# Rows for the PE inside and behind the expert mixing, early row fetches on POOL, and reordered evacuations and softmax products in a two-block transformer kernel

## What is computed

```python
q = (h @ wq).reshape(B, S, 8, 2, 128)
sub_scores = einsum('bshpk,hpnk->bshpn', q, subkeys)      # 2 x 128 scores for each head
top_v, top_i = top_k(sub_scores, 16)
cand = top_v[..., 0, :, None] + top_v[..., 1, None, :]    # 256 candidates
best_v, best_pos = top_k(cand, 16)                        # 16 of 16384 experts
gates = softmax(best_v)
hid = gelu(einsum('tkd,td->tk', u[expert], x)) * gates
out = einsum('tk,tkd->td', hid, v[expert])
```

## Time and profile before

| | |
|---|---|
| median of 3 runs | 3134.32 us (3134.2 to 3149.95) |
| the profiled execution, its own time | 3133.42 us |
| its span | 3131.7 us |
| PE busy | 2735.1 us, 87% |
| PE weight loads | 2092.0 us, 67% |
| DVE busy | 1690.6 us, 54% |
| ACT busy | 898.5 us, 29% |
| POOL busy | 1306.2 us, 42% |
| moved by DMA | 584.37 MB, mean 187 GB/s |
| mean granted clock of TensorE | 0.941 of full speed |

### The profile page before, as it was taken

One profiled execution on the slowest core, in us unless ns is written; L12 is line 12 of the kernel. 1 busy time (PEld: TensorE's weight loads), 2 busy tenths in 40 slices (PEclk: granted clock), 3 DMA queues, 4 the chain that ended last, 5 costly groups with the idle time before them and its releaser, 6 DMA issues.

```text
span 3131.7 us, 32456 instructions
## 1 busy us (share of the span) xinstructions
PE 2735.1 (87%) x12138; PEld 2092.0 (67%) x12138; DVE 1690.6 (54%) x3212; ACT 898.5 (29%) x1634; POOL 1306.2 (42%) x979
## 2 busy tenths in 40 slices
PE   7989997899997889999896789999999799999800
PEld 6856886678787668887775678888888644444300
DVE  1032044843225244340315646999966999666699
ACT  3264244423334232222325233111113920000000
POOL 3422434634445224434342132344444544444574
PEclk9999998999998999999998799999999999999955
DMA  4300332013233116563331032899999089999997
GB/s 152 100 7 21 95 93 69 1 41 94 81 114 122 54 47 208 175 194 115 88 96 47 1 108 98 311 388 391 383 366 399 1 300 380 403 409 410 409 408 285
DMA packets 216990, 584.37 MB, mean 187 GB/s; under 512 B 23921, under 2 KB 48642, under 8 KB 216322
## 3 DMA queue, kind: packets, MB, share of 16 engines
q1 hardware_dynamic: 137312, 301.22, 28.2%
q0 software_dynamic: 74688, 271.61, 22.2%
q10 hardware_dynamic: 4834, 9.46, 0.9%
HBM read 574.88 MB, written 7.35 MB: 186 GB/s over the span
## 4 chain that ended last, share of the span: by engine, by line
PE 63%; DVE 13%; DMA 11%; issue 5%; ACT 4%; POOL 4%; SPq 0%; DVEq 0%; ACTq 0%; POOLq 0%
PE ps L1152 13%; PE ps L1154 13%; PE ps L1153 13%; PE ps L1601 12%; DMA rows<-in_v,expert 5%; DMA rows<-in_u,expert 5%; POOL rows L1086 3%; DVE ps L2256 1%; PE ps L1118 1%; DVE hg L2285 1%; DVE hot L2274 1%; PE ps L1230 1%; DVE rows L2244 1%; PE ps L1170 1%; PE ps L1168 1%
## 5 line engine op out<-in xcount | busy, mean ns | idle before, releaser
L991 POOL TENSOR_TENSOR wlo<-wraw,whi 128x1024 fp32r<-128x1024 f32 x258 | 621.3, 2415 | 974.0 <-ACT whi L543 973.9
L543 ACT ACTIVATE whi<-wraw 128x1024 fp32r<-128x1024 f32 x258 | 271.1, 1058 | 852.3 <-PE ps L1154 747.8
L1626 PE MATMUL ps<-stream,hg 128*128 128x512 f32 x1024 | 441.8, 594 | 7.7 <-DMA stream<-in_v 6.9
L1152 PE MATMUL ps<-hhi,whi 128*128 128x512 f32 x1096 | 431.8, 394 | 18.9 <-DVE hlo L1735 6.7
L1601 PE MATMUL ps<-haff,stream 128*128 128x256 f32 x2048 | 444.1, 380 | 2.2 <-ACT stg L928 2.2
L1154 PE MATMUL ps<-hhi,wlo 128*128 128x512 f32 x1096 | 429.4, 392 | 0.0
L1153 PE MATMUL ps<-hlo,whi 128*128 128x512 f32 x1096 | 429.0, 391 | 0.0
L1601 PEld LDWEIGHTS ps<-haff,stream 128*128 128x128 f32 x2048 | 390.1, 191 | 55.7 <-ACT stg L928 2.4
L1626 PEld LDWEIGHTS ps<-stream,hg 128*128 128x128 f32 x1024 | 195.1, 191 | 253.8 <-issue 245.1
L2244 DVE CUSTOM_DVE_ANT_0 rows<-rows,h_s 128x1024 f32<-128x1024 f32 x256 | 313.5, 1225 | 83.6 <-DMA rows<-in_u,expert 78.1
L1086 POOL DMA_INDIRECT rows<-in_v,expert x256 | 244.8, 956 | 270.9 <-DVE ps L2256 119.1
(11 more groups left out here) (447 smaller groups left out, 4089.7 us busy)
## 6 DMA issues: line engine op xcount, KB each, us to landing
stream<-in_ut SPq DMA_DIRECT2D x128, 512.0 KB, 6.8
stream<-in_v SPq DMA_DIRECT2D x128, 512.0 KB, 6.8
wraw<-in_w_in SPq DMA_DIRECT2D x96, 512.0 KB, 3.6
wraw<-in_w_ada SPq DMA_DIRECT2D x48, 512.0 KB, 4.0
wraw<-in_w_gu SPq DMA_DIRECT2D x88, 256.0 KB, 3.8
wraw<-in_w_down SPq DMA_DIRECT2D x22, 512.0 KB, 3.5
wraw<-in_w_br_ssm SPq DMA_DIRECT2D x16, 512.0 KB, 3.5
wraw<-in_w_xkv SPq DMA_DIRECT2D x16, 512.0 KB, 4.2
```

The source lines that it names most:

```text
L543: act.activation(whi[:, n % WSLOTS, 0:kn, :], wraw[:, n % WSLOTS, 0:kn, :], ACT.Copy).then_inc(w_hi, 1)
L991: pool.tensor_tensor(wlo[:, n % WSLOTS, 0:kn, :], wraw[:, n % WSLOTS, 0:kn, :], whi[:, n % WSLOTS, 0:kn, :].bitcast(F32), ALU.subtract).th ...
L1152: pe.matmul(dst, lh, rh, start=k == 0, stop=False)
L1626: ins = pe.matmul(ps[:, 2 * i + half, :], hg[:, n, P * i:P * i + P], stream[j][:, 4 * half:4 * half + 4, :], start=n == 0, stop=n == NKEYS ...
```

## The change

The sixteen rows of block 12 (v of tile 0), of which the ring holds eight when the hole begins, are handled by the PE inside the hole: a diagonal matrix of the token weights times the row buffer, in two halves of 512 columns, every fourth batch a whole row. ACT makes the first four diagonals between the gelus of dense tiles 126 and 127, DVE the other twelve between batches, and POOL issues fetches between its one-hots, for which it has four buffers of its own. In blocks 28, 30 and 31 the odd ranks are handled by the PE in the same way, with diagonals by ACT, while DVE sums the even ones; tile 0 and the dense tiles are finished after block 28, their root and scaling stand between later rows, and tile 1 alone is behind the last row. Modulation vector 5 moves from behind `gu10` to behind `gu4`. The memory is transposed to the banks of `mix0`, and `xk0`, `xk1` are evacuated before parts of the normalization of x. The cross-attention issues scores three tiles ahead. In the sliding window ACT makes diagonals of the reciprocals, and a matmul with them takes the place of multiplication and transpose. On POOL, `after("pq0")`, the first eight fetches and `after("pq3")` replace `after("pq3")`; the loads of the dense tiles' scores follow.

```diff
-GELU_AT = {21: 0, 40: 1, 66: 2, 91: 3, 110: 4}
+GELU_AT = {21: 0, 40: 1, 66: 2, 91: 3, 107: 4, 118: 5}
+PE_HOLE = [(12, k) for k in range(TOPK)]
+PE_TAIL = [(b, k) for b in (28, 30, 31) for k in range(1, TOPK, 2)]
+DIAGS, POOL_HOTS = 4, 4
+ENDS = (0, 2, 3, 1)
+VECTORS = [(i,) for i in range(4)] + [(4, 5)] + [(i,) for i in range(6, 12)]
...
             for i in range(NT):
                 u_root_of(i)
+            group(G["xk0"], (0, 1), to_features(kx, 0, n=MEM))
             for i in range(NT):
                 x_square(1, i)
+            group(G["xk1"], (0, 1), to_features(kx, 4, n=MEM))
             for i in range(NT):
                 x_root_of(i)
-            for i in range(2):
-                group(G[f"xk{i}"], (0, 1), to_features(kx, 4 * i, n=MEM))
...
+            def sw_diagonals(b):
+                act.wait_ge(s("sw_rec"), b + 1)
+                if b:
+                    act.wait_ge(s("sw_tr"), 4 * b)
+                for h in range(SW_HEADS):
+                    act.activation(sw_dg[:, h, :], ident, ACT.Copy, scale=srec[:, h:h + 1]).then_inc(s("sw_p"), 1)
...
+            def row_diags(mine):
+                for b, k in mine:
+                    r = PE_ROWS.index((b, k))
+                    act.wait_ge(s("wrow_ready"), PE_BLOCKS.index(b) + 1)
+                    if r >= DIAGS:
+                        act.wait_ge(s("pe_row_used"), r - DIAGS + 1)
+                    n = TOPK * BLOCKS[b][2] + k
+                    act.activation(diag[:, r % DIAGS, :], ident, ACT.Copy, scale=wrow[:, n:n + 1]).then_inc(s("diag_ready"), 1)
...
+                if n == NKEYS - 2 and PE_HOLE:
+                    row_diags(PE_HOLE[:DIAGS])
...
+            if PE_TAIL:
+                row_diags(PE_TAIL[:8])
+                tile_squares((0, 1, 2))
+                row_diags(PE_TAIL[8:16])
+            row_gelu(1, PEER_HEADS - 1)
...
             after("out1")
-            after("pq3")
-
+            after("pq0")
...
+            for n in range(RING):
+                gather_next()
+            after("pq3")
             load_scores(0)
             load_scores(1)
-            for b, (kind, t, h) in enumerate(BLOCKS):
-                if kind == "u":
-                    pool.wait_ge(s("head_done"), top_done(t, h))
+            for b in range(len(BLOCKS)):
                 for k in range(TOPK):
                     if k == RING and b == MIX_AFTER + 1:
                         pool.wait_ge(s("slots_ready"), 1)
                         for m in range(ND // 4):
                             first_hot(m)
+                            if PE_HOLE and m % 4 == 0 and m > 4:
+                                gather_next()
...
-            xa_scores(0)
+            for i in range(3):
+                xa_scores(i)
...
+                    pe.wait_ge(s("sw_p"), SW_HEADS * b + 2 * n + 2)
                     for m in range(4):
...
-                        ins = transpose(ps[:, 4 + n, P * m:P * m + P], sw_ss[b % 2][:, q // 2, P * (q % 2):P * (q % 2) + P])
+                        ins = pe.matmul(ps[:, 4 + n, P * m:P * m + P], sw_ss[b % 2][:, q // 2, P * (q % 2):P * (q % 2) + P], sw_dg[:, q // 2, :], start=True, stop=True)
...
+            def row_half(r, half):
+                b, k = PE_ROWS[r]
+                mine = [n for n, (c, _) in enumerate(PE_ROWS) if BLOCKS[c][1] == BLOCKS[b][1]]
+                j, count = row_count(b, k)
+                if half == 0:
+                    pe.wait_ge(row_landed[j], 16 * count)
+                    pe.wait_ge(s("diag_ready"), r + 1)
+                return pe.matmul(ps[:, 6 + half, :], diag[:, r % DIAGS, :], rows[j][:, 512 * half:512 * half + 512], start=r == mine[0], stop=r == mine[-1])
...
+                if PE_HOLE and b % 4 == 1:
+                    row_half(b // 4, 0)
+                if PE_HOLE and b % 4 == 3:
+                    row_half(b // 4, 1).then_inc(s("pe_row_used"), 1)
...
+            def hole_diagonal(r):
+                b, k = PE_HOLE[r]
+                n = TOPK * BLOCKS[b][2] + k
+                v.wait_ge(s("pe_row_used"), r - DIAGS + 1)
+                v.tensor_scalar(diag[:, r % DIAGS, :], ident, wrow[:, n:n + 1], None, ALU.mult).then_inc(s("diag_ready"), 1)
...
+            between_rows = {(28, 14): lambda: later_weights(30), (30, 2): lambda: later_weights(31),
+                            (30, 8): lambda: root_begin((0, 1, 2)), (30, 14): lambda: root_end((0, 1, 2)),
+                            (31, 2): lambda: scaled_out((0,)), (31, 4): lambda: scaled_out((1,)), (31, 6): lambda: scaled_out((2,))}
...
                 if b == MIX_AFTER:
+                    if PE_HOLE:
+                        head_weights(*BLOCKS[PE_HOLE[0][0]][1:]).then_inc(s("wrow_ready"), 1)
...
+            if PE_TAIL:
+                link(add_tile(1, own_sums(1)))
+                v.wait_ge(s("pe_row_used"), len(PE_ROWS))
+                add_tile(1, row_sums(1)).then_inc(x_ready, 1)
```

More of the change, by code:

```diff
@@ L969, in scalar_program @@
                 row_gelu(0, h)
-            for h in range(PEER_HEADS):
+            for h in range(PEER_HEADS - 1):
                 row_gelu(1, h)
-            for i, t in enumerate((0, 2, 3, 1)):
-                act.wait_ge(x_ready, NT * 4 + i + 1)
-                act.activation(yout[:, t, :], xf[:, t, :], ACT.Square, accum_out=ssq[:, t:t + 1]).then_inc(usq_ready, 1)
-            act.wait_ge(usq_ready, part_count(4, 0, NT - 1))
-            root(meps)
+            if PE_TAIL:
[3 more added lines that the diff above has]
+            row_gelu(1, PEER_HEADS - 1)
+            if not PE_TAIL:
+                tile_squares((0, 1, 2, 3))
+            tile_root((0, 1, 2))
+            row_diags(PE_TAIL[16:])
+            if PE_TAIL:
+                tile_squares((3,))
+            tile_root((3,))
         def gpsimd_program(pool):
@@ L1366, in tensor_program @@
             pe.wait_ge(s("memn_ready"), 2)
-            evacuated("mix1")
+            evacuated("mix0")
             for k in range(KD):
                 for i in range(2):
-                    ins = transpose(ps[:, k, P * i:P * i + P], mem_n[:, i, P * k:P * k + P])
-                ins.then_inc(s("mtr_ready"), 1)
+                    ins = transpose(mem_t(k)[:, P * i:P * i + P], mem_n[:, i, P * k:P * k + P])
+                if k % 2:
+                    ins.then_inc(s("mtr_ready"), 1)
             pe.wait_ge(s("m_lo"), KD)
@@ L1628, in tensor_program @@
                 ins.then_inc(s("v_mm"), 1)
+            for r in range(len(PE_HOLE), len(PE_ROWS)):
+                row_half(r, 0)
+                row_half(r, 1).then_inc(s("pe_row_used"), 1)
         def vector_program(v):
```

243 lines of the change are left out of this document (155 added, 88 removed).

## The result

| | before | after |
|---|---|---|
| median of 20 runs | 3143.43 us (3133.87 to 3149.95) | 3125.78 us (3114.69 to 3134.67) |
| profiled execution, its span | 3131.7 us | 3118.6 us |

The ratio is 0.9948, with a 95% interval of 0.9934 to 0.9961: about 16 us faster, where 33 were forecast and the range ended at 3118. The direction was right, the size was not. Of the three runs that the prediction had of the kernel before, two (3134.2 and 3134.32 us) are among the fastest of its twenty and one (3149.95) is the slowest; the profiled execution, 3133.42 us, is faster than all twenty.

A forecast was written before the change was run, and what follows sets the result against it. It took PE to bound the kernel before about 1970 us and DMA to be full in the last 1150 us except the hole. Terms summed to -33.4 us, from 3133.42 to 3100.0 us, range 3080 to 3118.

The forecast's parts named there:

- memory and xk: Memory and cross-attention: earlier mem transposes, xk0 and xk1 evacuated first; -8 us (-2 to -10).
- the attention: Cross-attention: with three score tiles ahead, scores leave the turn for tiles 1 and 2; -3.3 us (-2 to -5).
- the stall at pq2: Start of pq2: PE idles 6.3 us for POOL's low part, then 1.9 more; +8.2 us (5 to 11).
- the hole's start: Start of the hole: ACT's four diagonals delay slot_t from 2415.37 to 2418.4; +3 us (0 to 5).
- length: Inside the hole: PE's row halves and DVE's twelve diagonals lengthen it; +5.5 us (2 to 15).
- the sliding window: Sliding window: DVE loses its multiplication, ACT gains diagonals, k_out's transposes start earlier; -12 us (-8 to -14).
- The hole's yield: After the hole: DVE stands 16 rows further on; -20.5 us (-18 if only the 14 fetches issued inside count).
- the tail: Last blocks: 14 us saved behind the last fetch, last landing slips 7 to 10; -6 us (-14 to +4).
- the early rows pay: Rival at pq and the DMA-bound stretches: eight early rows gain 10.3 us without PE stall; 3081.5 us, chance 0.06.
- the hole eats its yield: Rival in the hole: every half costs PE's whole 0.5 us, start and length +20.5; 3112 us, chance 0.14.
- TensorE's lower clock: Rival in the tail: TensorE at 1.2 GHz, a row 3.4 us on PE; 3117 us, chance 0.08.
- The slow hole: Rival: TensorE stays at 1.2 GHz through the hole, PE needs 170 us there; 3165 us, chance 0.03.

The follow-up runs named there:

- the first experiment: Changed kernel with the eight early fetches issued behind pq3's low parts; median 3123.97 us, span 9.6 us less once corrected for a differing start.
- the third experiment: Changed kernel with no rows for PE in the hole; median 3131.24 us, span 10.4 us more once corrected for a differing start.
- second experiment: Changed kernel with no rows for PE in blocks 28, 30, 31; median 3126.83 us, span 2.6 us less once corrected for a differing start.
- The seventh experiment: Changed kernel with u rows of blocks 27 and 29 multiplied by a token copy in PSUM; median 3117.68 us, beside 3131.35 for the changed kernel.
- the tenth experiment: The mended kernel with gelus of heads 3, 4, 5 behind dense tiles 88, 105, 117 instead of 91, 107, 118; median 3092.73 us.
- the mended kernel: Changed kernel with later early fetches, block 30's last gelu earlier, PSUM token in blocks 27 and 29, six adds spread through block 28; median 3109.0 us.
- 9: Kernel before with 32 unread tile copies added to ACT's program in the sliding window; median 3190.37 us, beside 3195.79 for the kernel before.
- 12: Kernel before with the changed kernel's GELU_AT alone, second run; 3182.98 us beside 3191.09 for the kernel before, ratio given as 0.9987.

## Why the prediction was right and wrong

**Right, to 2.5 us:** memory and xk (-10.5 for -8, just past the end of its range), the attention (-5.1 for -3.3), the stall at pq2 (6.22 for 6.3 us, +8.5 for +8.2), no gain from early rows (the first experiment), the hole's start (+2.7 for +3) and length (+4.3 for +5.5).

**Right in kind, off in size:** the sliding window, -7.9 for -12. The forecast's chain was 4 us too short; PE waits 4 to 6 us for ACT's diagonals in each block, and which link was too short wasn't looked for. The hole's yield, -16.5 for -20.5: the rows gave 17.7 us by the third experiment, as the forecast had it if only the fetches issued in the hole count (-18), and 1.1 us is lost without them too.

**Wrong: the tail.** The step that failed is "last landing slips 7 to 10 us. -6 (-14 to +4)". The saving behind the last fetch was right, 12.6 us for 14, and so were the two causes it named: the adds behind block 28, and the weights of (30, 2) "whose gelu stands on ACT behind diagonals". But the slip was 26.2 us, and the tail +13.6. The forecast took each fetch at 1.28 us and never asked what POOL's issue takes beside a DVE that is no longer waiting for landings. Its own text tells of DVE and POOL taking turns at the ports where DVE has two operands in SBUF, but it used this for DVE's small instructions beside POOL's subtractions and didn't turn it round. And it put at nothing that DVE now adds all its rows to one sum, 1.39 us a row where a landing takes 1.28, which is what the traces show ahead of the full ring of block 27.

Block 27 cost 6.1 us more. Block 29 cost 8.7: without the tail's rows (second experiment) it cost 4.0, and the other 4.7 came with the adds behind block 28. The seventh experiment took both blocks back to 20.4 and 20.7 us and lost 3.2 in block 28. Block 30 cost 9.6, and moving one gelu gave 6.0 of the whole back.

Of the rivals, "the early rows pay" falls with the first experiment, "the hole eats its yield" with the third (10.4 us net). TensorE's lower clock did come in the tail, but each time only for the first rows behind a pause: the granted clock is 0.50 from 3003 to 3012, from 3054.5 to 3060 and from 3078 to 3083.5, and 0.57 from 3097 to 3101, with 3.68 to 3.78 us for the first row; between these it is 0.98 to 1.00, and the last row took 1.98 us. In the changed kernel POOL waits for no PE row in blocks 28 to 31, and ahead of row (30, 7) PE stood 0.86 us until the row landed. So the clock isn't what held the fetches there. The slow hole didn't come: granted clock 0.98. None of the rivals is what cost the tail its time.

A second fault lay ahead of the sum: it was made against a profiled execution that was one of the fastest of the kernel before. Against the median of twenty, the same -33 would have given 3110; so 10 of the 25.8 us between the forecast and the measured median come from this. A third is a reading: DMA was not full all through the last 1150 us. In the kernel before it moved 336 GB/s from 2255 to 2295, around the wait for the gelu of tile 91, and the tenth experiment, which moves that gelu in the mended kernel, gained 4.6 us.

**Open.** Where the kernel before takes 3180 us and more, it and its two variants run there (experiments 9 and 12) stand still on ACT at about the 96th dense tile and again between the 111th and the 117th, and lose 41 us. In the first of these stops the DMA is full of row fetches. A shift of ACT's program by 32 instructions didn't change it (9), nor did the places of the gelus (12). No version with the changed kernel's other parts showed it; their dense u took 443 to 445 us. What ACT waits for is not in the records, and which part of the change spares it wasn't found.

## What to carry to other kernels

When a change takes away the gaps of an engine that waits for landings, price again every instruction of its neighbours that used these gaps; here 0.1 us more for each row was enough to fill the ring. A queue that issues fetches is worth keeping clear of the ports of its neighbour; one operand moved to PSUM, with one copy of the token for each of two blocks, gave back 12.9 us. And an order on one engine that mixes paced work (diagonals, one for each row) with a single result that another engine needs should have the single result first.

## What the runs showed of the hardware

- POOL's indirect fetch issue takes 0.94 us beside DVE products with one operand in PSUM that start every 1.14 us. Beside products with both operands in SBUF it takes 0.94 to 0.99 us if they start every 1.28 us, and 1.99 us if they start every 1.15 us.
- The DVE product of 128 x 1024 takes 1.22 us with its second operand in SBUF or in PSUM.
- DVE's multiply and add of a 128 x 1024 row into PSUM came every 1.39 us with one sum and every 1.20 us with two sums in turn, with the rows landed in both cases.
- The same code at 188 to 235 us ran at a granted clock of 0.89 in one execution and 1.00 in another. The two were 9.5 us apart at the last product of the first attention, and the profiles of all kernels here spread over 15.7 us at that point.
- The gain of a change can depend on the chip: 0.9948 where the kernel before ran its dense u stage in 444 us, 0.9827 where it took 485.
